# Cross-attention: the turn of the probabilities as a product with a diagonal matrix of reciprocal sums

## The reference

```python
def cross_attention(x, mem_k, mem_v, w_q, w_o):
    B, T, _ = x.shape
    q = (x @ w_q).reshape(B, T, H_X, HEAD_DIM).astype(F32)
    s = jnp.einsum('bthd,bmhd->bhtm', q, mem_k.astype(F32)) * HEAD_DIM ** -0.5
    p = jax.nn.softmax(s, axis=-1)
    o = jnp.einsum('bhtm,bmhd->bthd', p, mem_v.astype(F32)).reshape(B, T, D_X)
    return o.astype(x.dtype) @ w_o
```

## Time and profile before

| what | value |
|---|---|
| median of 3 runs | 2680.47 us |
| the 3 runs | 2672.03, 2681.99, 2680.47 us |
| profiled execution, its time | 2674.92 us |
| its span in the profile | 2673.0 us |
| granted TensorE clock, mean over the span | 0.975 |
| PE busy | 2548.0 us, 95% |
| PEld busy | 2441.2 us, 91% |
| DVE busy | 1054.5 us, 39% |
| ACT busy | 585.5 us, 22% |
| POOL busy | 1541.5 us, 58% |

### The profile page before, as it was taken

How to read it: one execution, slowest core, us unless ns; L and a number is a source line. 1 busy time by engine, 2 the same in 40 slices (tenths; PEclk the granted TensorE clock), 3 DMA queues, 4 the chain that set the end, 5 groups by cost and what they waited for, 6 DMA issues and landing times.

```text
span 2673.0 us, 47936 instructions
## 1 busy us (share of the span) xinstructions
PE 2548.0 (95%) x18450; PEld 2441.2 (91%) x18450; DVE 1054.5 (39%) x1597; ACT 585.5 (22%) x1100; POOL 1541.5 (58%) x1877
## 2 busy tenths in 40 slices
PE   7999999999987999999999999999999879999997
PEld 7999999988776899999899999999787768999997
DVE  3222225654547622222422222257345576222224
ACT  2000004322325500000310000143223254000004
POOL 8866662733248776666486666536231578766641
PEclk9999999989999999999999999999889989999999
DMA  6322220212012132222132222202120131322201
GB/s 229 119 79 86 78 86 9 80 48 91 33 56 97 63 104 87 78 86 79 40 121 80 83 82 83 74 17 80 40 84 32 64 97 64 103 87 78 86 32 36
DMA packets 61099, 203.99 MB, mean 76 GB/s; under 512 B 6808, under 2 KB 13976, under 8 KB 60312
## 3 DMA queue, kind: packets, MB, share of 16 engines
q1 hardware_dynamic: 52288, 184.83, 20.3%
q10 hardware_dynamic: 8664, 17.17, 1.8%
HBM read 195.66 MB, written 7.88 MB: 76 GB/s over the span
## 4 chain that ended last, share of the span: by engine, by line
PE 83%; DVE 8%; POOL 3%; issue 3%; ACT 2%; DMA 0%; ACTq 0%; DVEq 0%; POOLq 0%; SPq 0%
PE pairA L401 22%; PE pairD L401 20%; PE pairB L401 19%; PE pairD L410 8%; PE pairA L410 2%; PE pairB L410 2%; POOL scratch L2172 1%; POOL w L2139 1%; PE pairD L671 1%; PE pairD L673 1%; DVE scratch L1815 1%; DVE y L1637 1%; PE pairD L793 0%; DVE prx L2101 0%; PE pairB L828 0%
## 5 line engine op out<-in xcount | busy, mean ns | idle before, releaser
L2139 POOL TENSOR_TENSOR w<-w_raw,w 128x256 fp32r<-128x256 f32 x1372 | 1043.3, 791 | 28.6
L2132 POOL TENSOR_SCALAR w<-w_raw 128x1024 fp32r<-128x1024 f32 x343 | 365.2, 1065 | 815.9 <-issue 456.7
L401 PE MATMUL pairA<-x_hi,w 128*128 128x288 f32 x3136 | 571.0, 300 | 3.6 <-DVE scratch L1567 2.7
L401 PE MATMUL pairB<-x_hi,w 128*128 128x288 f32 x2752 | 497.4, 298 | 0.0
L401 PE MATMUL pairD<-h_hi,w 128*128 128x288 f32 x2688 | 480.1, 298 | 14.1 <-DVE kw L1905 4.3
L401 PEld LDWEIGHTS pairA<-x_hi,w 128*128 128x128 f32 x3136 | 474.3, 192 | 7.2 <-issue 6.3
L401 PEld LDWEIGHTS pairD<-h_hi,w 128*128 128x128 f32 x2688 | 402.9, 190 | 17.1 <-issue 6.3
L401 PEld LDWEIGHTS pairB<-x_hi,w 128*128 128x128 f32 x2752 | 414.2, 191 | 1.1 <-issue 0.2
L1612 DVE TENSOR_TENSOR y<-y,pairD 128x576 f32<-128x576 f32 x256 | 193.1, 754 | 561.4 <-PE pairD L401 561.4
L401 PE MATMUL pairA<-x_lo,w 128*128 128x288 f32 x1568 | 339.2, 298 | 0.0
L401 PE MATMUL pairB<-x_lo,w 128*128 128x288 f32 x1376 | 297.1, 298 | 0.0
(11 more groups left out here) (335 smaller groups left out, 2905.9 us busy)
## 6 DMA issues: line engine op xcount, KB each, us to landing
w_raw<-in_stream SPq DMA_DIRECT2D x348, 512.0 KB, 3.4
out_ak<-pa ACTq DMA_DIRECT2D x2, 1152.0 KB, 4.2
out_y<-y SPq DMA_DIRECT2D x8, 288.0 KB, 2.2
mem_raw<-in_mem ACTq DMA_DIRECT2D x2, 1024.0 KB, 4.8
cst<-in_consts ACTq DMA_DIRECT2D x1, 1740.0 KB, 8.2
tb_dram<-in_rel ACTq DMA_DIRECT2D x2, 768.0 KB
y<-in_x ACTq DMA_DIRECT2D x2, 576.0 KB, 7.3
y<-in_x ACTq DMA_DIRECT2D x1, 1152.0 KB, 11.4
```

Source lines behind the costliest of these rows:

```text
L401: ins.append(mm(out[0:m, half, 0:n], wt, mv_[:, c:c + n], start=(start and i == 0), stop=(stop and i == 2)))
L2132: pool.tensor_scalar(hi, w_raw[:, j], 1.0, 0.0, ALU.mult, ALU.add).then_inc(unit_hi, 1)
L2139: i_ = pool.tensor_tensor(lo[:, b], w_raw[:, j, b], hi[:, b].bitcast(F32), ALU.subtract)
```

## The change

The scaling of the probabilities on DVE is replaced by the making of a diagonal matrix, and the turn on PE by an ordinary product with that matrix. For each head DVE multiplies the identity by the reciprocal sums, one for each partition, into `sil[b]`; PE multiplies `prx` transposed by it, which turns and scales in one product. `prx` is no longer written by DVE.

```diff
@@ x_turn(t), on PE
                     for h in range(NH):
                         for k in range(2):
                             c = (h % 2) * NMEM + k * P
-                            i = nc.tensor.transpose(out[:, h // 2, c:c + m], prx[0:m, t % 2, h, k * P:k * P + P],
-                                                    ident[0:m, 0:m])
+                            i = mm(out[:, h // 2, c:c + m], prx[0:m, t % 2, h, k * P:k * P + P],
+                                   sil[t % 2][0:m, h * P:h * P + m], start=True, stop=True)
@@ x_probs(t), on DVE
                     step(v.reciprocal(rc_x[0:m, NH * b:NH * b + NH], sm_x[0:m, NH * b:NH * b + NH]))
                     for h in range(NH):
-                        i = v.tensor_scalar(prx[0:m, b, h, :], prx[0:m, b, h, :], rc_x[0:m, NH * b + h:NH * b + h + 1],
-                                            None, ALU.mult)
+                        i = v.tensor_scalar(sil[b][0:m, h * P:h * P + m], ident[0:m, 0:m],
+                                            rc_x[0:m, NH * b + h:NH * b + h + 1], None, ALU.mult)
                         inc(i, dve_step) if h < NH - 1 else step(i, E("x.probs"))
```

## The result

The changed kernel has a median of 2685.62 us over 20 runs (2669.38 to 2692.78); the kernel before has 2675.39 us over 20 runs. The ratio is 1.0035, with a 95% interval from 1.0022 to 1.0047, which is +9.4 us. That is within the 0.5% that was forecast as "the same", and the time is 0.4 us from the forecast.

What follows compares the result with a forecast made beforehand. PE bounds the kernel (95% busy, 83% of the chain). PE +8.9, DVE -0.8 and clock -0.6 sum to +7.5 us; with a base between profiled execution and median, 2686 us, own range 2679 to 2694.

Steps and rivals of the forecast that it cites:

- Two instructions for each product: PE's turn: an fp32 product issues two instructions, a transpose one; 16 matmuls a turn instead of 8, chance 0.72.
- Rival 3: PE's turn: the product goes in one pass or the doubling is hidden; only DVE's -0.8 us left, 2679 us, chance 0.06.
- The pitch: PE's turn at full clock: 0.117 us per instruction, old or new; eight more add 0.9 us to a turn.
- Rivals 4 and 5: PE's turn: weight load no longer hidden, 2703 us, chance 0.05; each product costs four transposes, 2704 us, chance 0.03.
- The turn of tile 0: PE, begun at half clock: eight more instructions add 0.9 us in the first layer, 1.8 in the second.
- The turn of tile 4: PE, last tile: grows 0.56 us, of which some 0.3 show behind ACT's copy; 0.6 us for both layers.
- DVE: Scalings of tiles 1 and 2: narrow operations still wait for POOL, saving 0.2 us a tile, -0.8 us in all.
- contended scalings under 2.5 us: Sign against the forecast: DVE's four operations beside POOL, expected at 2.8 to 3.1 us, falling below 2.5.
- rival 2: DVE's narrow operations slip between POOL's, saving 2.2 us a tile, 8.8 in all; 2679 us, chance 0.10.
- The clock: Granted clock in the tiles' stage, the loose term: taken as 0 to -1.3 us, so -0.6.
- The fall in the second layer's stage: Half clock at tile 2's values, 2.88 us instead of 1.58; if missed, 1.3 us come back.
- Rival 6: Half clock for most of the stage: a turn of 16 takes 3.6 us, 2698 us, chance 0.04.

Runs made afterwards that it cites:

- E3: The kernel before with every transpose issued twice, 16 in a turn, same output; ratio to before 1.0004, +7.6 us at equal clock.
- E6: The changed kernel with probabilities and diagonals held as fp32r, so the product takes one pass; ratio to before 1.0017, -3.0 us at equal clock.
- E5: The changed kernel measured again, nothing altered; ratio to before 1.0038, +9.2 us at equal clock.
- E1: The kernel before with only the PE half: turn as fp32 product with the identity, DVE scaling as before; ratio 1.0021, +10.0 us at equal clock.
- E7: The changed kernel with a tile's four diagonals made by one DVE operation of 512 columns; ratio to before 1.0008, +2.3 us at equal clock.
- E4: The kernel before with one DVE scaling of 1024 columns for a tile in place of four of 256; ratio 0.9959, -3.6 us at equal clock.
- E9: The kernel before with one DVE scaling of 1024 columns for a tile, measured on another run of the chip; ratio 0.9979, -3.6 us at equal clock.
- E8: The changed kernel with fp32r operands for the turn and one DVE diagonal operation for a tile; ratio to before 0.9974, -6.1 us at equal clock.

## Why the prediction was right, point by point

- **Two instructions for each product: right.** 160 matmuls, and E3 (twice as many transposes) and E6 (the product in one pass) show that the number is what costs. Rival 3 falls with it.
- **The pitch (the distance between two starts): right.** 0.112 us for an instruction was measured, against an estimate of 0.113 from L518 and 0.117 from the turns. Tiles 1 to 3 grew by 0.96 us each where 0.9 was said. Rivals 4 and 5 fall with it.
- **The turn of tile 0: the size depends on the clock.** The forecast had +0.9 in the first layer and +1.8 in the second. Measured are 3.72 us in both, +1.8 each: the forecast took the half clock of the first layer to end where it had ended before, after 3.4 us, and it lasted 6.8. In E5 it lasted 3.4 and the turn was 2.77 us, +0.9.
- **The turn of tile 4: mis-sized.** The sentence "the pitch is 0.07 and eight more are 0.56" took the pitch of the old instructions for 64 columns. The product's pitch is 0.112 for 64 columns as for 128 (1.94 us in all, E3 has 1.15), so the turn grew by 1.2 us in place of 0.56, and ACT's copy of that tile began 2.0 us after the turn's start (886.49 - 884.52) in place of 1.0. That is about 1.0 us for a layer in place of 0.3. A term of 0.6 us should have been 2.0.
- **DVE: right in size, and one meeting with POOL not foreseen.** The narrow operations wait as the wide ones did. Against E1, which has wide operations and the same turns, they are 0.23 and 0.21 us shorter, the 0.2 that was said, and the whole change is 0.8 us faster at equal clock. Against the kernel before, the chain gained 0.25 us in tile 1 and 0.67 in tile 2, for both layers 1.8; the other 1.0 comes with PE's half, after which DVE's operations fall differently against POOL's, and the forecast had no term for it. It changes from run to run: in E5's first layer tile 2 took 2.73 us and not 2.35. The prediction had named contended scalings under 2.5 us as a sign against itself. Tile 2 is under it, by this shift and not by the relief of rival 2 (2.2 us for a tile), which falls.
- **The clock: the direction was open, and stays so.** The fall in the second layer's stage is gone, as half expected; in its place L518 ran at half clock in both layers (4.38 for 2.69), a place that the forecast had not named. In E5 it did so in the second layer alone (2.69 and 4.37), in E7 in both (4.21 and 4.28). Rival 6 falls: 6.8 us of a stage of 43.3 were at half clock. Which stretches get half clock changes from kernel to kernel and from run to run, and I can't say what this change in particular does to it.

Without the clock the terms as forecast were 8.9 - 0.8 = 8.1 us; with tile 4 at 2.0, tile 0 at +0.9 to +1.8 and DVE at its measured sizes they are 5.8 + 2.0 + 1.8 to 3.6 - 1.8, which is 7.8 to 9.6, and 9.2 were measured. The mechanism was right. That the time came within 0.4 us is luck: the forecast of 2686 rested on a base of 2678.5, between the median and the profiled execution, and the base turned out to be 2675.4, 3.1 lower, while the 7.5 us of the change were 2.7 too few by the medians (10.2). One sum is not consistent: rivals 2 and 3 are put at 2679, reckoned from the median of 2680.5, and from the forecast's own base they would be 2677.3 and 2677.7.

What the experiments found besides: the number of DVE operations beside POOL was a cost on this path already before the change, and the change leaves it at four. A version that beats both kernels at full precision is E4: -3.6 us at equal clock in two sets, with intervals of the plain ratio of 0.9941 to 0.9977 and 0.9962 to 0.9995.

## What to carry to other kernels

A call in the program is not one instruction on the engine: compare counts in the trace with counts in the program before costing a product that replaces a transpose. Where two engines keep each other waiting operation by operation, fewer operations help more than narrower ones: here half the width saved 0.2 us for a tile, and one operation in place of four 1.2 to 1.3 in the tiles that met POOL before. And where the granted clock differs between runs, compare lines of time against clock, or stretches of the trace, before believing a difference of a few tenths of a per cent.

## What the runs showed of the hardware that was not expected

- The instructions of an ordinary fp32 product with weights of 128 columns start 0.112 us apart (the median), whether 128 or 64 columns are moved, and in fp32r it is the same (8 in 1.02 us for 64 columns). A transpose of 64 columns has a pitch of 0.062. The weight loads of the product are recorded with 192 ns, those of the transposes with 140; that the load sets the pitch fits this, but was not tried by itself.
- One tensor_tensor of 1024 columns on DVE takes 1.22 us alone and up to 2.13 beside POOL (E4, E9), four tensor_scalar of 256 take 1.14 and 3.20. In E4 it is the rest of the one POOL operation that runs when DVE's begins, and then 1.07 to 1.08 us; POOL's four of 256 columns take 3.62 us behind it in place of 2.78.
- Half clock at the same place of the stage lasted 3.4 or 6.8 us in runs of one kernel (E5, first and second layer), and 10.2 us in all four stages of the two kernels with the fp32r product (E6, E8). Why is not shown.
- The time of one kernel on one core spreads over 20 us (2669.38 to 2692.78), and follows the mean granted clock at 1.9 to 2.7 us for each 0.001.
